# Spreading compressed attention over the pairs of the main attention, with a rebuilt start and later bank claims, in a three-mixer transformer kernel

## The reference, cut to what matters

```python
# start: first norm, then one wide projection
hn = rms_norm(h, mix_norm_pre[l]); proj = hn @ w_in[l]
# third mixer
q = rms_norm_2(proj[..., :NSA_Q_WIDTH].reshape(B, S, NSA_HEADS, NSA_HEAD_DIM), q_norm)  # 16 heads of 64
q_rope = apply_rope_2(q, cos, sin)          # k_sel, k_win: normed with k_norm[1], k_norm[2] and rotated
kc = rms_norm_2(compress(k_cmp, ...), k_norm[0]); vc = compress(v_cmp, ...)              # 31 compressed keys
s_c = einsum(qp, kc) * scale;  p_c = masked_softmax(s_c, cmp_end <= t);  o_c = p_c @ vc  # compressed
# selected and window branches: with 8 blocks and 16 picks every block is picked,
# so both are causal attention over all keys
o = g[:, :, 0] * o_c + g[:, :, 1] * o_s + g[:, :, 2] * o_w
```

## Time and profile before

| | us |
|---|---|
| median of 3 runs | 2307.42 (2306.75 to 2307.64) |
| the profiled execution, its time | 2307.61 |
| the profiled execution, its span | 2305.8 |
| PE busy | 2135.4 (93%) |
| DVE busy | 1261.0 (55%) |
| ACT busy | 808.6 (35%) |
| POOL busy | 91.8 (4%) |
| mean granted clock of PE | 0.962 of full speed |

### The profile page before, as it was taken

The page is one execution under the profiler, slowest core; times in us unless marked ns, Lnnn a source line. Parts: engine busy times, 40 slices in busy tenths (PEclk is TensorE's granted clock), DMA queues, the critical chain, the costliest instruction groups (busy, mean ns, idle before and its releaser), DMA issues.

```text
span 2305.8 us, 28424 instructions
## 1 busy us (share of the span) xinstructions
PE 2135.4 (93%) x10880; PEld 1738.8 (75%) x10880; DVE 1261.0 (55%) x2209; ACT 808.6 (35%) x1467; POOL 91.8 (4%) x88
## 2 busy tenths in 40 slices
PE   4998898999899899999999999999669999999998
PEld 3876576888788688887788877779546667888787
DVE  2578447777654423683755545664566756322234
ACT  3333445333323435213422222333236644222232
POOL 0002300000000010000000000000210110000000
PEclk8999899999999899999999999999779999999999
DMA  4321113556442132101465636323300013422221
GB/s 150 110 73 55 37 56 119 183 183 190 139 162 94 65 95 98 46 1 56 134 204 168 197 117 211 119 64 95 103 1 2 2 38 117 137 94 92 92 92 55
DMA packets 146642, 233.10 MB, mean 101 GB/s; under 512 B 7276, under 2 KB 83532, under 8 KB 146252
## 3 DMA queue, kind: packets, MB, share of 16 engines
q1 hardware_dynamic: 142304, 222.28, 29.9%
q10 hardware_dynamic: 3340, 5.85, 0.7%
q0 software_dynamic: 864, 3.15, 0.4%
HBM read 229.16 MB, written 2.10 MB: 100 GB/s over the span
## 4 chain that ended last, share of the span: by engine, by line
PE 78%; DVE 12%; ACT 4%; issue 4%; POOL 1%; DMA 0%; ACTq 0%; DVEq 0%; POOLq 0%
PE ps L2096 10%; PE ps L2098 10%; PE ps L2097 10%; PE ps L2121 4%; PE ps L2363 4%; PE ps L2122 4%; PE ps L2123 4%; PE ps L2280 4%; PE ps L2056 4%; PE ps L2058 4%; PE ps L2057 4%; PE ps L2282 3%; PE ps L2142 3%; PE ps L2154 2%; PE ps L2167 2%
## 5 line engine op out<-in xcount | busy, mean ns | idle before, releaser
L1512 DVE TENSOR_TENSOR w_lo<-ring,w_hi 128x1024 fp32r<-128x1024 f32 (+4 forms) x362 | 376.5, 1041 | 795.9 <-ACT w_hi L946 795.2
L946 ACT ACTIVATE w_hi<-ring 128x1024 fp32r<-128x1024 f32 (+4 forms) x362 | 329.5, 912 | 992.3 <-PE ps L2098 467.3
L2096 PE MATMUL ps<-x_hi,w_hi 128*128 128x512 f32 x1056 | 415.9, 394 | 0.0
L2098 PE MATMUL ps<-x_hi,w_lo 128*128 128x512 f32 x1056 | 411.2, 389 | 0.0
L2097 PE MATMUL ps<-x_lo,w_hi 128*128 128x512 f32 x1056 | 410.8, 389 | 0.0
L2097 PEld LDWEIGHTS ps<-x_lo,w_hi 128*128 128x128 f32 x1056 | 198.3, 188 | 42.7 <-issue 1.9
L2096 PEld LDWEIGHTS ps<-x_hi,w_hi 128*128 128x128 f32 x1056 | 198.3, 188 | 42.3 <-issue 1.9
L2098 PEld LDWEIGHTS ps<-x_hi,w_lo 128*128 128x128 f32 x1056 | 198.2, 188 | 41.7
L2121 PE MATMUL ps<-w_hi,x_hi 128*128 128x512 f32 x480 | 187.5, 391 | 3.7 <-DVE x_hi L1586 3.7
L2123 PE MATMUL ps<-w_hi,x_hi 128*128 128x512 f32 x480 | 186.8, 389 | 0.0
L2122 PE MATMUL ps<-w_lo,x_hi 128*128 128x512 f32 x480 | 186.8, 389 | 0.0
(11 more groups left out here) (308 smaller groups left out, 3148.8 us busy)
## 6 DMA issues: line engine op xcount, KB each, us to landing
ring<-in_ada_w SPq DMA_DIRECT2D x48, 1024.0 KB, 5.2
ring<-in_ffn_w_in SPq DMA_DIRECT2D x88, 512.0 KB, 4.6
ring<-in_w_up SPq DMA_DIRECT2D x44, 512.0 KB, 4.4
ring<-in_ffn_w_out SPq DMA_DIRECT2D x20, 1024.0 KB, 4.9
ring<-in_hgrn_w_in SPq DMA_DIRECT2D x16, 1024.0 KB, 5.1
ring<-in_w_in SPq DMA_DIRECT2D x12, 1024.0 KB, 5.0
ring<-in_w_down SPq DMA_DIRECT2D x10, 1024.0 KB, 4.9
ring<-in_kv_ada_w SPq DMA_DIRECT2D x8, 1024.0 KB, 5.1
```

The lines of the kernel that those rows point to most:

```text
L946: a.activation(to[:, n % depth, 0:src.shape[-1]], src, ACT.Copy).then_inc(s["hi_done"], 1)
L1512: v.tensor_tensor(to[:, n % depth, 0:width], src, hi[:, n % depth, 0:width].bitcast(F32), ALU.subtract).then_inc(s["lo_done"], 1)
L2096: mm(bs[j], wh[:, k, c], x_hi[:, 2 * q + k], start=first, stop=False)
L2098: ins = mm(bs[j], wl[:, k, c], x_hi[:, 2 * q + k], start=False, stop=last)
```

## The change

It has four parts.

1. **Start.** x comes in four transfers, one for each token tile, and SP issues them ahead of the weights, with no wait. SP issues 17 other loads (`load_constants`) between the first and the second weight unit. ACT keeps the identity (a cut of `small`) and the six groups of norm rows. PE turns the norm rows at once and the other rows after the third piece of the first projection (`other_rows`, bank 7), DVE copies these and the masks after the fourth. The norm goes by tile; two pieces of the first weights are split ahead of the turned input (`EARLY[0]`), and DVE no longer waits for the last turned tile.
2. **Feed-forward.** PE opens each down bank at its first use. DVE does the last modulation rows (`ada_out`) before `up_gated`.
3. **Preparation.** POOL multiplies the norm weights into rotation tables once (`rope_g`, 12 small products, and one for `cmp_norm`), after the second kvs unit. The keys' four chunks are rotated by DVE during the query projections (`k_chunk` after pieces (nq 0, 7), (nq 1, 1), (nq 1, 7), (nq 2, 1)). The queries' eight chunks are turned by PE between the four parts of `cmp1`, `cmp2` and `cmpT`, in the order `PREP`; POOL has no part in them. The plain and the rotated chunk are turned both.
4. **Compressed attention** has no loop of its own: group i takes steps 7i to 7i + 6 of the main attention, all of its PSUM through bank 7, one after the other. B of the main attention keeps to bank 6. Tiles run from the last to the first.

```diff
 # the plan
-                plan_bank((name, "B", g), 6 + g % 2)
+                plan_bank((name, "B", g), 6 + (g % 2 if name == "dsa" else 0))
+        Q_CHUNKS = [(t, j) for t in reversed(range(NT)) for j in range(2)]
+        PREP = [("cmp1", 0, 0), ("q", 0), ("cmp1", 0, 1), ("q", 1), ("cmp1", 1, 0), ("q", 2), ("cmp1", 1, 1), ("q", 3), ("cmp2",),
+                ("q", 4), ("q", 5), ("cmpT",), ("q", 6), ("q", 7)]
-        GROUPS = [(t, kp) for t in range(NT) for kp in range(2)]
-        for i in range(len(GROUPS) + 2):
-            if i < len(GROUPS):
-                plan_bank(("cS", i), i % 4)
-            if 1 <= i <= len(GROUPS):
-                plan_bank(("cT", i - 1), 4 + i % 2)
-            if i >= 2:
-                plan_bank(("cO", i - 2), 6 + i % 2)
+        GROUPS = [(t, kp) for t in reversed(range(NT)) for kp in range(2)]
+        for i in range(len(GROUPS)):
+            for kind in ("cS", "cT", "cO"):
+                plan_bank((kind, i), 7)
+        def cmp_step(j, at):
+            i, step = divmod(j, 7)
+            return i if step == at and i < len(GROUPS) else None
+        EARLY[0] = [(("iq", q), "iq", q * PIECE, PIECE) for q in range(2)]
 # SP
-            sp.wait_ge(s["x_in"], 16)
+            for t in range(NT):
+                sp.dma_start(x_tok[:, t], io["x"][0, t * P:(t + 1) * P, :]).then_inc(s[f"x_in{t}"], 16)
             for n, (pieces, _) in enumerate(units):
+                if n == 1:
+                    load_constants()
 # POOL
+            evacuated(pool, ("kvs", 1, NT - 1))
+            pool.wait_ge(s["consts_in"], 32)
+            pool.wait_ge(s["cmp_pos_in"], 64)
+            for j in range(3):
+                gain = qk_norm[:, j, :].rearrange("p (q d) -> p q d", q=2)
+                cos, sin, nsin = [rope_t[:, i] for i in range(3)]
+                for q in range(2):
+                    g.tensor_tensor(rope_g[:, j, :, 32 * q:32 * q + 32], cos, gain[:, q:q + 1].broadcast_to([P, NT, HD // 2]), ALU.mult)\
+                        .then_inc(s["tables_done"], 1)
...
-            for t in range(NT):
-                for j in range(3):
-                    i = 3 * t + j
-                    pool.wait_ge(s["raw_norm"], i + 1)
...
 # ACT
             def norm(i):
 
                 if i == 0:
-                    act.wait_ge(s["x_in"], 16)
                     for t in range(NT):
+                        act.wait_ge(s[f"x_in{t}"], 16)
                         x_rms(0, t)
+                    early_highs(0, slice(0, 2))
+                    evacuated(act, "vec")
                 norm_out(i)
...
+            def cmp_between(i):
+                if i % 2 or i == 0:
+                    return
+                j = i // 2 - 1
+                n = cmp_step(j, 2)
+                if n is not None:
+                    act.wait_ge(s["cmp_l"], n + 1)
+                    if n >= 2:
+                        filled(act, ("cT", n - 2))
+                    a.activation(cp[:, n % 2, :, 0:NCMP], cl[:, n % 2], ACT.Exp, scale=SCALE).then_inc(s["cmp_p"], 1)
+                n = cmp_step(j, 4)
...
 # DVE
-                    if i == 0:
-                        filled(dve, ("xT", 0, KT - 1))
                     for kt in range(KT):
+                        if i == 0 and kt in (0, 2):
+                            early_lows(0, slice(kt // 2, kt // 2 + 1))
...
-                up_gated(i, FFN_UNITS - 1)
                 for u in (FFN_UNITS - 2, FFN_UNITS - 1):
                     for mj in ada_after.get((i, u), []):
                         ada_out(*mj)
+                up_gated(i, FFN_UNITS - 1)
...
+            def q_chunk(i):
+                t, j = Q_CHUNKS[i]
+                dve.wait_ge(s["raw_norm"], 2 * i + 2)
+                if i >= 2:
+                    filled(dve, ("nT", i - 2, 1))
+                rope_gained(n_a[:, i % 2], t, 0, n_b[:, i % 2], n_o[:, i % 2], 8)
+                if i + 1 < len(Q_CHUNKS):
+                    q_norm(i + 1)
+                after()
+                v.tensor_tensor(n_o[:, i % 2], n_b[:, i % 2], n_o[:, i % 2], ALU.add).then_inc(s["rope2_done"], 1)
+            def cmp_between(i):
+                if i % 2 or i == 0:
+                    return
+                for at, part in ((1, cmp_logits), (3, cmp_factors), (6, cmp_result)):
+                    n = cmp_step(i // 2 - 1, at)
+                    if n is not None:
+                        part(n)
...
 # PE
-                bs = [open_bank(("down", i, j)) for j in range(8)]
+                bs = [None] * 8
...
+                    if k == 0:
+                        bs[2 * t + half] = open_bank(("down", i, 2 * t + half))
...
+            def cmp_between(j):
+                i = cmp_step(j, 0)
+                if i is not None:
+                    t, kp = GROUPS[i]
+                    b = open_bank(("cS", i))
...
+                i = cmp_step(j, 3)
+                if i is not None:
+                    pe.wait_ge(s["cmp_p"], i + 1)
...
+                i = cmp_step(j, 5)
+                if i is not None:
+                    t, kp = GROUPS[i]
+                    evacuated(pe, ("cT", i))
...
```

More of the change, by code:

```diff
@@ L1259, in _ @@
+            attention("nsa", cmp_between)
             sqrt_table()
@@ new lines, in cmp_second @@
+            def cmp_second():
+                for kv in range(2):
+                    for j in range(2):
+                        evacuated(pe, ("cmp1", kv, j))
+                pe.wait_ge(s["w2_in"], 32)
+                b = open_bank("cmp2")
+                for kv in range(2):
+                    for kh in range(NSA_KV):
+                        for n in range(2):
+                            ins = mm(b[0:NCMP, kv * 256 + kh * HD:kv * 256 + (kh + 1) * HD], h1[:, kv, n, kh], w2_sb[:, kv, n, :],
+                                     start=(n == 0), stop=(n == 1))
+                ins.then_inc(full("cmp2"), 1)
@@ new lines, in _ @@
+            for what in PREP:
+                if what[0] == "cmp1":
+                    cmp_first(what[1], what[2])
+                elif what[0] == "q":
+                    q_turn(what[1])
+                elif what[0] == "cmp2":
+                    cmp_second()
+                else:
+                    cmp_turn()
+            for t in range(NT):
+                evacuated(pe, ("kT", t))
+            for i in range(len(Q_CHUNKS)):
+                for n in range(2):
+                    evacuated(pe, ("nT", i, n))
```

463 lines of the change are left out of this document (239 added, 224 removed).

## The result

| | before | after |
|---|---|---|
| median of the runs, us | 2307.09 (2305.27 to 2307.64, 4 runs) | 2244.84 (2244.26 to 2245.27, 4 runs) |
| span of the profiled execution, us | 2305.8 | 2243.5 |
| PE busy, us | 2135.4 | 2127.3 |
| mean granted clock of PE | 0.962 | 0.971 |

A forecast was written before the change was run, and what follows sets the result against it. PE was taken to bound the kernel, so gains come from its idle time and half clock. Start 25, feed-forward 18 and third mixer 35.2 sum to 78.2 us off 2307.61, forecast 2229 us, range 2219 to 2249.

The forecast's parts named there:

- two tiles stand at 18.3. The projection starts at about 18.4: Start: with two split tiles ready at 18.3, the first projection begins at about 18.4 instead of 42.42, 24.0 us earlier.
- rival (a): Start: loads bound it and the projection starts at 29; 11 us less gain, 2240; chance 0.11.
- the 2.5 us for the clock: Start, first projection: about a dozen matmuls no longer at half clock, 0.23 us each instead of 0.44, gain 2.5 us.
- a row: Start: the profile page's first slice shows clock 0.8 with PE mostly idle; by it the 2.5 us would come.
- rival (c): Feed-forward: down parts are held by high and low pieces, not banks; a third of 18 us comes, 2241; chance 0.06.
- a chunk waits for the turn of the last but one: Preparation, query chunks after the first two: PE sets 4.8 us per chunk, so the fourth comes at 1646.5.
- then DVE is the chain: Preparation after cmp2 at 1648.5: DVE's compressed-key steps, 5.0 us, and chunks 5 to 7 set the end, 1661.5 before the last turn.
- rival (b): Compressed attention: one bank makes PE wait 1 us at each of 24 handovers; 21.5 us less gain, 2251; chance 0.09.
- (d): Compressed attention: a whole step lost at each of 24 bank handovers; at 3.6 us each the kernel is slower, 2313; chance 0.02.
- PE's part: Compressed attention among the pairs: eight groups of 2.29 us PE work, 18.3, minus 1.0 for logits in the filling.
- VectorE's stalls: Compressed attention: five groups cost no wait; the last three, among short tiles, cost 2.5 us in all, bounds 0 and 7.
- slices 31 and 32: Profile page before the change: besides the first slice, the only ones of 40 with PE under nine tenths busy; clock falls too.

The follow-up runs named there:

- The run with later chunks: Changed kernel with the four key chunks one to five pieces later among the low pieces; 2242.05 us, ratio 0.9712.
- The run with early chunks: Changed kernel with query chunks reordered, chunks 0 and 1 made before the last projection results and turned ahead of cmp1; 2238.92 us, ratio 0.9703.
- the pair of runs: Changed kernel plus norm rows in bank 7, seven groups' VectorE portions behind, early query chunks, later roots: 2222.0 us; the same with compressed attention in its own loop: 2226.00.

## Why the forecast was right in kind and 15.8 us off

**Start: 15.9 instead of 25.** The step that failed is "two tiles stand at 18.3. The projection starts at about 18.4": between the two nothing was counted but the split tiles. The bank was left out. The turned norm rows took bank 0 in the rotation, so the eighth turned tile stood in the bank of the projection's first product, and PE had to wait for its copy, 6.1 us behind the second split tile. The run that moves the norm rows to bank 7 shows it. Of the 9.1 us that were missing it gives back 8.2 by the first down part (8.6 by medians): 5.4 are the wait for the bank, 1.6 the half clock behind it, the rest isn't placed. A second, smaller term was mis-sized, the loads: x's last tile landed at 12.5 instead of 10.4, the weights at 15.0 instead of 13.3, and even with the bank free the projection starts at 20.7 instead of 18.4. So rival (a), which had the projection at 29 for the loads' sake, is near the measured 26.1 by number only: the loads make 2.3 us of the 7.7 by which it is late, and the bank 5.4.

Of the 2.5 us for the clock, 1.0 came in the changed kernel (eight matmuls at 0.43 instead of thirteen), and nearly all in the run with the other bank. The prediction set a row against the Trainium skill, TensorE: Matmul & The Clock Gate, Part 1, which says that an idle PE runs at half rate by default and that activity releases it. The trace agrees with the page: the first turns follow each other at 0.21 us, in the bank run the later ones at 0.11, and after 6.67 us of idleness the projection is at half clock again, after 1.65 it is not. The row was misread: its first slice counts as full what lies before the first recorded stretch of the clock, so its 0.8 says nothing of an idle PE. That the 2.5 us were right for the bank run is due to the turns, which the prediction named too, and not to the row.

**Feed-forward: 16.5 instead of 18**, and 18.1 alone on the kernel before. All three down parts follow without idle time. Mechanism and size hold; rival (c) falls.

**Keys: 1.0 instead of 0.8.** VectorE's first key chunk waited 1.53 us for the last table product, and PE 0.7 for the low piece behind it. The run with later chunks takes the wait away; what that brings is within the scatter. The Trainium skill, GPSIMD Engine Reference, section 1, says that GpSimd shares its SBUF interface with VectorE. The trace agrees in kind: the chunk's norm took 0.99 us beside the products and 0.68 without them. By that rule the prediction gave 2.4 us, which did not come: all 13 products took 6.9 us, near the 6.2 worked out from their size and not 8.

**Preparation: 55.4 instead of 55.8.** From PE's end of the projections to the main attention it is 42.3 us (1595.2 to 1637.5); 42.0 were worked out (1621.0 to 1663.0), and the steps inside fit too: the fourth query chunk is turned 26.2 us after that beginning, and 25.5 were worked out. That "a chunk waits for the turn of the last but one" is seen in VectorE's waits of 1.81 us, and "then DVE is the chain" in PE's 4.53. The run with early chunks shows what the prediction didn't ask: two of VectorE's eight chunks fit into its idle time ahead of the last results (4.55 us). No run undoes the preparation's change alone: of the 55.4 us, 24.6 are the compressed attention that went elsewhere, and the other 31 are read from the traces.

**Compressed attention among the pairs: 24.5 instead of 19.8.** The mechanism held: the three products are never late, so rival (b) with its bank handovers fell, and (d) with it. Two terms were small. PE's part was put at 17.3 (18.3 less 1.0 in the filling) and is 19.3: the filling, to the first values' products, grew from 11.7 to 12.6 us, since the first logits take 2.07 in it at half clock, and then come seven times 1.0, eight times 0.37 and eight times 1.06, 18.4; a group is 2.43 and not 2.29. VectorE's stalls were put at 2.5, in the last three groups; they are 5.3 from the third group on, ten waits of PE over 0.2 us where before it had none. The prediction counted VectorE's free time per step and not where in a step the portion stands: ahead of the softmax steps that free PE's bank, and twice right behind a group's end. Moving seven groups' portions behind these steps took 2.7 us of waits away. So, as changed, the spreading gave nothing: 24.5 us among the pairs against the 24.6 of a stage of its own, and the run that undoes it is no slower. It pays only once VectorE's order is right: 3.3 us by stretches and 4.0 by medians in the pair of runs, 1.9 to 2.2 where the clock is alike.

**A reading.** The hole of the earlier trace rows that the prediction calls slices 31 and 32 is slices 29 and 30, 1614 to 1729 us. Nothing was worked out from the numbers of the slices.

**Open.** Executions differ by 2 to 3 us up to the first down part in kernels with the same code there, and no run tells why. In the attention the difference of 1.1 to 1.5 us goes with the clock at its start, which stays at half for 6.3 us in the changed kernel and for 3.3 to 3.8 in three others; why it rises sooner there isn't shown.

## What to carry to other kernels

When an order of work changes, list for each product the bank that it writes and who reads it last, before any load is costed: one bank at the start took some 8 us of a gain of 25. Work spread into another loop costs waits by its place: here it belonged behind the step that frees the bottleneck's next buffer, except in the last group, where behind was too late for the next engine. The average slack of the engine says nothing about that. A wait in the queue of an engine holds everything behind it, so what is needed last is asked for last.

## What the runs showed of the hardware

The clock can fall after a short wait, and the same wait doesn't always bring it about. A wait of 1.68 us among short products was followed by products of 2.08 where 1.13 is usual, and by a granted clock of 0.66 over 10 us; a wait of 1.43 was followed by a clock of 0.72 over 6 us in one run, and one of 1.44 at the same place of another run by no fall. Seven waits of 0.43 to 1.39 us in the changed kernel's attention weren't followed by one either. At the start, 1.65 us of idleness (the run with the other bank) left the clock full, and 6.67 us (the changed kernel) were followed by eight matmuls at 0.43 instead of 0.23.

A granted clock of 1.00 ahead of the first recorded change is no measurement. At the start of the traces it says 1.00, while the first turns follow each other at 0.21 us, twice the 0.11 of later; the pace of like instructions is the check.
